# Changes of stage at 512 tokens: x and context accumulated in separate banks, x finished first, the next stage's first four tiles in two passes

## The reference

```python
for layer in range(2):
    x   = x   + 0.5 * mx[2] * swiglu(rms_norm(x)   * (1 + mx[1]) + mx[0], ffn1_gu, ffn1_down)
    ctx = ctx + 0.5 * mc[2] * swiglu(rms_norm(ctx) * (1 + mc[1]) + mc[0], ffn1_gu, ffn1_down)
    hx = rms_norm(x)   * (1 + mx[4]) + mx[3];   hc = rms_norm(ctx) * (1 + mc[4]) + mc[3]
    # hx @ w_in: q, k, v, pool, fft; hc the same (in the last layer only k, v)
    x   = x + mx[5] * (mixers(hx, hc) @ w_out)
    x   = x + 0.5 * mx[8] * swiglu(rms_norm(x) * (1 + mx[7]) + mx[6], ffn2_gu, ffn2_down)
    if layer == 0:
        ctx = ctx + mc[5] * (mixers(hc) @ w_out);   ctx = ctx + ... swiglu(...) as for x
# mx, mc = silu(c) @ ada_w + ada_b: the conditioning, nine groups a layer
```

## Time and profile before

| | us |
|---|---|
| median of 3 runs | 2786.44 |
| lowest, highest | 2783.71, 2787.35 |
| the profiled execution | 2785.05 |
| its span, first to last instruction | 2783.3 |

### The profile page before, as it was taken

One profiled execution on the slowest core, in us unless ns is written; L12 is line 12 of the kernel. 1 busy time (PEld: TensorE's weight loads), 2 busy tenths in 40 slices (PEclk: granted clock), 3 DMA queues, 4 the chain that ended last, 5 costly groups with the idle time before them and its releaser, 6 DMA issues. The chain is left out here.

```text
span 2783.3 us, 46152 instructions
## 1 busy us (share of the span) xinstructions
PE 2719.9 (98%) x17972; PEld 2430.3 (87%) x17972; DVE 1774.8 (64%) x2333; ACT 1202.5 (43%) x1757; POOL 202.1 (7%) x224
## 2 busy tenths in 40 slices
PE   7999999999999999999999999999999999999998
PEld 4888887788888878888879998999899999998998
DVE  4777535767772377742765568875476577668874
ACT  3233233642332232321555456554554445456553
POOL 1000012000000000000200014000200000004000
PEclk9999999999999999999999999999999999999999
DMA  6565532025663255543326643565456566653564
GB/s 255 189 189 189 166 108 76 16 94 190 190 187 104 83 161 190 187 143 98 123 103 196 197 155 110 177 202 176 146 178 204 177 202 216 202 175 109 183 200 136
DMA packets 153530, 444.07 MB, mean 160 GB/s; under 512 B 46528, under 2 KB 47936, under 8 KB 152768
## 3 DMA queue, kind: packets, MB, share of 16 engines
q1 hardware_dynamic: 119248, 431.38, 47.2%
q0 software_dynamic: 1008, 10.75, 1.0%
q10 hardware_dynamic: 33152, 0.26, 0.7%
HBM read 441.16 MB, written 1.18 MB: 159 GB/s over the span
## 5 line engine op out<-in xcount | busy, mean ns | idle before, releaser
L1726 DVE TENSOR_TENSOR wlo<-raw,whi 128x1024 fp32r<-128x1024 f32 x672 | 831.3, 1240 | 575.6 <-ACT whi L1220 572.8
L1220 ACT ACTIVATE whi<-raw 128x1024 fp32r<-128x1024 f32 x672 | 708.3, 1056 | 626.1 <-PE ps L573 575.4
L571 PE MATMUL ps<-nh,whi 128*128 128x512 f32 (+1 forms) x1280 | 498.4, 389 | 3.5 <-DVE nl L1791 1.7
L573 PE MATMUL ps<-nh,wlo 128*128 128x512 f32 (+1 forms) x1280 | 492.6, 385 | 0.0
L572 PE MATMUL ps<-nl,whi 128*128 128x512 f32 (+1 forms) x1280 | 492.6, 385 | 0.0
L571 PE MATMUL ps<-bh,whi 128*128 128x256 f32 x1456 | 405.9, 279 | 0.0
L572 PE MATMUL ps<-bl,whi 128*128 128x256 f32 x1456 | 404.6, 278 | 0.0
L573 PE MATMUL ps<-bh,wlo 128*128 128x256 f32 x1456 | 404.4, 278 | 0.0
L571 PEld LDWEIGHTS ps<-nh,whi 128*128 128x128 f32 x1280 | 241.2, 188 | 72.8 <-issue 12.6
L573 PEld LDWEIGHTS ps<-nh,wlo 128*128 128x128 f32 x1280 | 241.2, 188 | 48.1
L571 PE MATMUL ps<-mh,whi 128*128 (+1 forms) x1024 | 282.8, 276 | 0.0
(11 more groups left out here) (257 smaller groups left out, 4205.4 us busy)
## 6 DMA issues: line engine op xcount, KB each, us to landing
raw<-stream SPq DMA_DIRECT2D x800, 512.0 KB, 3.4
head<-stream SPq DMA_DIRECT2D x8, 1024.0 KB, 14.6
gates_w<-gate_in POOLq DMA_DIRECT2D x2, 3328.0 KB, 13.0
cst<-cst_in POOLq DMA_DIRECT2D x2, 1280.0 KB, 6.0
X<-x_in SPq DMA_DIRECT2D x1, 2048.0 KB, 7.8
out<-X SPq DMA_DIRECT2D x8, 128.0 KB, 2.0
fftw<-fftw_in POOLq DMA_DIRECT2D x2, 256.0 KB, 5.9
ws<-ws_in POOLq DMA_DIRECT2D x1, 512.0 KB, 3.9
```

The costliest lines, as they stand in the source:

```text
L571: pe.matmul(dst, w1, rhs_hi, start=start, stop=False)
L573: return pe.matmul(dst, w2, rhs_hi, start=False, stop=stop)
L1220: act.activation(whi[:, at % RING, :], raw[:, n % RING, :], ACT.Copy).then_inc(w_hi_ready, 1)
L1726: dve.tensor_tensor(wlo[:, r, :], raw[:, PLACE["main", at] % RING, :], whi[:, r, :].bitcast(F32), ALU.subtract).then_inc(w_ready, 1)
```

## The change

1. **Down and out projections at T** issue each 512-wide product as two 256-wide ones. `half_bank(m, half)` puts `x` of output tile m in banks 0 to 3, the context in banks 4 to 7, two tiles in one bank. A slot runs all eight tiles for one half, then for the other (`slot_halves`; the first slot of a stage takes the context half first).
2. **The last two slots** (`last_two_halves`) finish all `x` tiles first, then the context in the order `TURN[1]`. Between context tiles PE sums the squares of `x` and spreads its root.
3. **The norm** runs for `x`, then for the context (`norm_halves` on DVE and ACT, `norm_squares` on POOL), with the context's additions set between the scalings of `x`.
4. **The next stage's first four tiles** (`first_tiles`) run on `x` columns, with the context's sums and root between tiles, and then on context columns. In `in0` the conditioning's sums come between the passes, and ACT's store and load of it, with the wait between them, after the context's norm.
5. `keep_busy` is gone from these changes. `hh` and `hl` move from `WIDE_AT` to `NARROW_AT`; `nh` and `nl` stay.

```diff
-        hh = sb("hh", [P, NF * T], F32R, line=WIDE_AT)
-        hl = sb("hl", [P, NF * T], F32R, line=WIDE_AT)
+        hh = sb("hh", [P, NF * T], F32R, line=NARROW_AT)
+        hl = sb("hl", [P, NF * T], F32R, line=NARROW_AT)
...
+TURN = [list(range(KD)), [6, 7, 2, 3, 0, 1, 4, 5]]
+        ROW_BANK = [7, 5]
+        def half_bank(m, half):
+            return ps[:, 4 * half + m // 2, m % 2 * S:(m % 2 + 1) * S]
...
+            def first_tiles(at, widths, context_sums=True, between=None):
+                weights(at + 1)
+                for k in range(KD):
+                    pe.wait_ge(nl_ready, base + k + 1)
+                    for n in range(2):
+                        one(n, k, 0)
+                if context_sums:
+                    norm_sums(1, 6)
+                for n in (2, 3):
+                    weights(at + n)
+                    for k in range(KD):
+                        one(n, k, 0)
+                    if n == 2 and context_sums:
+                        norm_rows(1)
+                if between:
+                    between()
+                for k in range(KD):
+                    pe.wait_ge(nl_ready, base + KD + k + 1)
+                    for n in range(2):
+                        last = one(n, k, 1)
+                        if k == KD - 1:
+                            last.then_inc(slots_done, 1 if n == 0 or widths[2] == T else 3)
+                for n in (2, 3):
+                    if widths[n] == T:
+                        for k in range(KD):
+                            last = one(n, k, 1)
+                        last.then_inc(slots_done, 1)
...
+            def slot_halves(at, dyn, src_h, src_l, first, evac=None):
+                for half in ((1, 0) if first else (0, 1)):
+                    part = slice(half * S, (half + 1) * S)
+                    for m in range(KD):
...
+                        ins = mm3(half_bank(m, half), at, m, src_h[:, part], src_l[:, part],
+                                  first and m % 2 == 0, False)
+                ins.then_inc(slots_done, 1)
+            def last_two_halves(at, src):
+                for half in range(2):
+                    for i, m in enumerate(TURN[half]):
+                        for n, (src_h, src_l) in enumerate(src):
...
+                            if half and i == KD - 1:
+                                last.then_inc(slots_done, 1)
+                        if i % 2 and not (half and i == KD - 1):
+                            last.then_inc(acc_done, 1)
+                        if half and i == 3:
+                            norm_sums(0, 0)
+                        if half and i == 5:
+                            pe.wait_ge(x_new, done + KD + 2)
+                            norm_rows(0)
...
-                norm(T, busy=(9 if l else 6, 2, 11))
-                norm(w, busy=(13 if l else 9, 2, 6 if l else 11))
+                if w == S:
+                    norm((13, 2, 6))
...
+            def norm_halves(at, ord_shift, begun=False, ada=False):   # ACT
+                after = {0: [4], 1: [5], 3: [6], 4: [7]}
+                    for i in range(KD):
+                        square(i, T)
+                    for i in range(4):
+                        square(i, T, 1)
+                    root(0)
+                for m in range(KD):
+                        for i in after.get(m, []):
+                            square(i, T, 1)
+                    upper(m, ord_shift, nh)
+                    if m in (5, 6):
+                        split_to(at + m - 3)
+                    root(1)
+                for m in range(KD):
+                    upper(m, ord_shift, nh, 1)
+                if ada:
+                    ada_rows(c["ada"], 0, head_row)
+                    ada_columns(c["ada"], 0)
...
+            def norm_halves(at, ord_shift, scale_at, name=None, gate=None):   # DVE
+                if name:
+                    for i in range(KD):
+                        added(i, 0)
+                    add_last(0)
+                    for i in range(4):
+                        added(i, 1)
+                    inv_of_sums(0, 0)
+                    added(4, 1)
+                scaled(0, scale_at)
+                added(5, 1)
+                scaled(1, scale_at)
+                lower(0, ord_shift, nh, nl)
+                for m in range(2, KD):
+                    scaled(m, scale_at)
+                    lower(m - 1, ord_shift, nh, nl)
+                    if m in (2, 3):
+                        added(4 + m, 1)
+                    if m == 5 and name:
+                        add_last(1)
+                lower(KD - 1, ord_shift, nh, nl)
+                split_to(at + 2)
+                if name:
+                    inv_of_sums(1, 6)
+                split_to(at + 3)
+                for m in range(KD):
+                    scaled(m, scale_at, 1)
+                    if m:
+                        lower(m - 1, ord_shift, nh, nl, 1)
+                lower(KD - 1, ord_shift, nh, nl, 1)
```

More of the change, by code:

```diff
@@ L578, in keep_busy, with norm, norm_sums, norm_rows @@
                     pe.matmul(bank(b, P), ones[:], ident[:], start=True, stop=True)
[L580 to L587, removed]
+            def norm(busy, split=True):
+                pe.wait_ge(x_new, x_count(c["norm"]) + 2)
+                keep_busy(1, busy[0])
+                norm_sums(0, 0)
+                keep_busy(1, busy[1])
+                norm_rows(0)
+                keep_busy(1, busy[2])
+                c["norm"] += 1
+                c["nl"] += KD if split else 0
+            def norm_sums(half, b):
+                c["sums"] += 1
+                pe.wait_ge(all_added, c["sums"])
+                for n in range(2 * half, 2 * half + 2):
+                    last = pe.matmul(ps[:, b, n:n + 1], sqsum[:, n * P:(n + 1) * P], ones[:, 0:1],
+                                     start=True, stop=True)
+                last.then_inc(sq_summed, 1)
+            def norm_rows(half):
                 c["rms"] += 1
                 c["root"] += 1
-                keep_busy(1, busy[1])
                 pe.wait_ge(rstd_ready, c["root"])
[L592 to L607, removed]
+                spread(tok_rstd, 2 * half, ROW_BANK[half], half * S).then_inc(rows_ready, 1)
+            def spread(cols, first, b, at=0):
+                for n in range(2):
                     last = pe.transpose(ps[:, b, at + n * P:at + (n + 1) * P],
-                                        cols[:, n:n + 1].to_broadcast([P, P]), ident[:])
+                                        cols[:, first + n:first + n + 1].to_broadcast([P, P]), ident[:])
                 return last
@@ L703, in ffn_up, with group @@
                 if ada_groups:
-                    def group(at, unit, g, done, i, tiles=8):
-                        for n in range(tiles):
+                    def group(at, unit, g, done, i, tiles=8, first=False):
+                        if first:
+                            pe.wait_ge(up_evac, unit + 2)
+                            first_tiles(at, [T] * 4, context_sums=at > 0)
+                        for n in range(4 if first else 0, tiles):
                             q = n // 2
@@ L969, in channel_dft, with conditioning @@
                     last.then_inc(f1_done, 1)
-                joint_tiles(bank(0), in_slot(l, 0), bank(1), in_slot(l, 1), 0, T)
-                for i in range(1, 9):
-                    if i > 1:
+                def conditioning():
+                    ada_sums(c["ada"], ACC[KD * c["ada"]] + KD, 0)
+                    c["ada"] += 1
+                first_tiles(in_slot(l, 0), [T, T, w, w], between=conditioning if l == 0 else None)
+                for i in range(2, 9):
+                    if i > 3:
                         tile(i)
@@ L1515, in _ @@
             act.activation(csil[:, :, 0:2], cvec[:], ACT.Silu).then_inc(csil_ready, 1)
-            for m in range(KD):
-                square(m, T)
-            squared()
+            for half in range(2):
+                for i in range(KD):
+                    square(i, T, half)
             act.preload_act_table(ACT.Sqrt)
             ada_rows(0, 0, head_row)
-            root(T)
+            root(0)
+            root(1)
             split_to(1)
@@ new lines, in scaled @@
+            def scaled(m, scale_at, half=0):
+                part = slice(half * S, (half + 1) * S)
+                if m == 0:
+                    c["rows"] += 1
+                    dve.wait_ge(rows_ready, c["rows"])
+                elif m >= 2:
+                    dve.wait_ge(nl_ready, c["y"] + m - 1)
+                dve.scalar_tensor_tensor(
+                    out=tmpb[:, m % 2, part], in0=X[:, m, part], scalar=fix[:, scale_at, m, half:half + 1],
+                    in1=ps[:, ROW_BANK[half], part], op0=ALU.mult, op1=ALU.mult).then_inc(y_ready, 1)
```

314 lines of the change are left out of this document (187 added, 127 removed).

## The result

| | before | after |
|---|---|---|
| median, us (lowest to highest, 15 runs each) | 2786.44 (2782.39 to 2790.64) | 2789.92 (2788.42 to 2795.10) |
| ratio to before | 1 | 1.0019, 95% interval 1.0011 to 1.0027 |
| span of the profiled execution, us | 2783.3 | 2787.9 |
| mean granted clock in it | 0.992 | 0.998 |
| three matmuls on `hh` (before 512 wide, after 2 x 256) | 0.68 us | 2 x 0.353 us |

The account below looks back on a forecast made before the run. PE, busy 98% of the span, was taken as the bound. Savings of 2.1 + 0.1 + 1.0 + 0.4 - 1.0 = 2.6 us took the profiled 2785.05 to 2782.5, the median to 2784; range 2775 to 2792.

Parts of the forecast that it names:

- The halves of `down` at no cost: Three down projections: 3168 matmuls of 256 at 0.1133 us replace 1584 of 512, cost 0, at most +21 us.
- the halves of `down` aren't half: Rival, down projections: shared banks or register addresses slow the halves; at 0.120 a matmul 21 us lost, 2805; chance 0.05.
- the rule on the gap: Skill's gap of N/2.4 + 2.5 ns between matmuls: halving `down` would cost 4 us more; not used in the sum.
- One change of stage: `ffn1_up1`, from the start of the last two slots to tile three's end: 40.75 us instead of 42.87, 2.1 saved.
- DVE gets through sooner: Rival, changes of stage: the `x` pass takes 7.3 us, each of four changes saves 1.9 more, 2776; chance 0.18.
- `in0`: Stage change where the conditioning's sums, 1 us of PE, lay in the wait before and now between passes; 1.0 saved.
- Its queue of store and load on ACT: `in0`: store and 3.1 us load waited for in a row on ACT; delays PE by 0, at worst 2.5 us.
- `ffn2_up0`: Stage change after the out projection: 2.1 us saved, less 1.9 of `out0`, about 0.1 net.
- `out0`: Out projection: 384 matmuls of 256 on wide `nh` cost 2.56 us, 0.64 of it in a wait; 1.9 lost.
- `in1`: Stage change whose tiles 2 and 3 lack context columns: tile 6 ends at 47.0 instead of 47.4 us, 0.4 saved.
- The head: `ffn1_up0`, no down projection before it: joint tiles before taken to end at 51.72, tile three at 62.6, now 63.6; 1.0 us lost.
- The clock: Rival, four changes of stage: without `keep_busy` the clock dips at the wrong place, 1.4 us each, 5.6 lost, 2789.5; chance 0.12.

Follow-up runs that it names:

- e1: Kernel before, with the 512-token down slots issued as two 256-column passes, each tile in its own bank, `hh` and `hl` at the narrow place; 2796.27 us, ratio 1.0048.
- e2: Kernel after, with the tiles of a slot ordered so no two neighbours share a bank, except in a stage's last two slots; 2791.81 us, ratio 1.0030.
- e8: Kernel after, with six useless fp32 matmuls ahead of each of the three 512-token down projections; 2783.38 us, ratio 0.9995.
- e9: Kernel after, with one useless 512-column matmul on the narrow-placed `hh` ahead of each 512-token down projection; 2781.19 us, ratio 0.9985.
- e10: Kernel before, with one useless 512-wide matmul from a wide place ahead of each S-wide down projection; 2799.55 us, ratio 1.0059.
- e7: TensorE alone, computation left out: one thing put between 512-wide matmuls on wide-placed `nh` and narrow 256-wide ones; 0.1133 to 0.1178 us a matmul, by what lay between.
- e5: TensorE alone multiplying zeros, computation left out, only the moving rows' place varied; 256 columns take 0.1133 us at 64 bytes past a multiple of 256, 0.1200 at 128.

## Why the prediction was wrong, point by point

**The halves of `down` at no cost: the step that failed.** I took 0.1133 from `nh_s` and bounded it by 0.1200. The pace was 0.1178, between the two: 3168 x 0.0044 = 14 us, of which the table shows 12.8. My rival "the halves of `down` aren't half" named the right place, but gave `hh` 0.120, two mechanisms (a shared bank, which e1 and e2 exclude, and register addresses, which e8 excludes, since it keeps them and has 0.1133), and a chance of 0.05. What I did not see is that each row I priced from had its own predecessor: the narrow 256-wide stages of the kernel before follow 256-wide work, and the new ones follow the 512-wide tiles of an up projection without a gap. The row showed the cost of an operation in its sequence, and I moved it into another. That the predecessors do it is shown (e8, e9, e10); why they do stays open. That the time is inside the range all the same is luck: beside the 2.6 that was forecast, 1.7 more at the changes of stage and some 4 by the clock (both below) hid two thirds of the loss.

The prediction's remark that the rule on the gap speaks against the change was right in sign only. By it (the Trainium skill, TensorE: Matmul & The Clock Gate, section Back-to-back issue gap) the spacing of 256 columns is, as an estimate, 256/2.4 + 2.5 = 109.2 ns; the traces have 113.3, 117.8 and 120.0 for the same 256 columns, so the measurement decides. And in e8 two halves take exactly what one whole takes before (2 x 0.1133 against 0.2267), so the rule's 4 us are not what was lost.

**One change of stage.** Right, nearly term by term (forecast, measured): wait for the sums 1.15, 0.77; for the spread 0.4, none marked; for the first `nl` 0.7, 0.47; end of the `x` pass 22.6, 22.4; context pass without a wait, so; end of tile three 40.75, 40.45. The stretch with `ffn1_up1` won 2.4 where 2.1 was said. (My list of what remains of the 8.1 us is short by 0.2: two sums of 0.47 are 0.94, not 0.75. The 40.75 has them right.) DVE's chain does bind the `x` pass; "DVE gets through sooner" did not come, though its waits were a little shorter.

**`in0`** won 1.4 us where 1.0 was said: its tile five starts 49.38 us after the last two slots began before, 48.00 after. Its queue of store and load on ACT cost nothing. **`ffn2_up0`** won 2.4 and `out0` lost 1.9 (forecast 2.1 and 1.9). **`in1`** ends tile six 47.6 us after the start, where 47.0 was said and 47.4 is before: no gain. Tile four's weights are there at 38.7, where 38.3 was worked out, and PE idles 1.0 and 1.1 around the two matmuls on `kqs` (L1090, L979 in the kernel before; forecast 1.1 and 1.7):

```profile
1369.50 0.28 PE L589 MATMUL ps<-nh,wlo 128*128 128x256 f32 x1
1370.78 1.10 PE L1090 MATMUL ps<-kqs,cst 128*128 128x512 f32 x2 [1.00 <-ACT kqs L1624]
1372.98 0.36 PE L587 MATMUL ps<-nh,whi 128*128 128x256 f32 x1 [1.11 <-DVE wlo L1866]
```

**The head** lost nothing, where I had 1.0. The term was mis-sized on the side of before: I read 51.72 as the last feature's end, but it is the start of its six matmuls, so the joint tiles end at 53.08 and tile three at 63.96. After has it at 63.81, near my 63.6. The last rows of tile nine, before and then after:

```profile
96.37 0.39 PE L573 MATMUL ps<-nh,wlo 128*128 128x512 f32 x1
```

```profile
96.25 0.39 PE L589 MATMUL ps<-nh,wlo 128*128 128x512 f32 x1
```

**The clock** went the other way from my rival: the changes of stage of the kernel after show 1.00 where those of before show 0.81, as real work fills what `keep_busy` filled with gaps around it. The dips on useless matmuls cost before next to nothing; what counts is where useful ones ran at the lower clock. From 455 to 475 it was 0.83 before and 0.91 after (3.4 and 1.8 us lost), and with the 2.7 from 1578 on that makes some 4 us in this pair of executions. So 12.8 were lost, 4.3 won at the changes of stage and in the head (1.4 + 0.5 + 2.4 - 0.2 + 0.1, forecast 2.6), and some 4 by the clock, which leaves the 4.5 of the span. Part of the clock's 4 is this pair's own: the profiled execution of e9 had the lower clock back (0.94 from 1960 to 2020), and the means over all executions, above, differ by 0.0016 only.

**In sum** the plan of the change is worth what the prediction said once the pace is mended, as far as the noise lets one say so: e9 is 0.15% faster than before (interval 0.06 to 0.24%), 3.7 us on the medians, with 0.8 us paid for its three breaks; the forecast was 2.6.

## What to carry to other kernels

The price of a matmul is read from a row whose predecessors are those of the new place, not only its shape and address: the paces for the same 256 columns differ by 4% with what ran ahead (0.1133 and 0.1178), and by 6% with the place (0.1133 and 0.1200). Where halving or reordering puts narrow matmuls behind wider ones, look at the first hundred of them in the trace, and where they come slowly, try one useless matmul between, of the form that worked here (512 columns from a narrow place). Filling a wait with the real work of the other half did for the clock here what useless matmuls did before.

## What the runs showed of the hardware

- The pace of a stream of 256-wide fp32r matmuls has a memory: 0.1133 or 0.1178 us at the same addresses, held over 1032 matmuls in the stage and over 96 with nothing else running. A single 512-wide matmul on a wide place sets the slow one in the midst of narrow 256-wide ones (e7, e10), but not behind six fp32 ones or 96 wide ones of 256 (e7). One wide matmul of 384 columns, one narrow 512, 24 wide 256 or two fp32 ones lift it, one or three fp32 ones don't (e7), and on `mh` it went after five matmuls by itself (e10). Why is open.
- The first byte of the moving rows past a multiple of 256 sets the pace too: for 256 columns 64 is best (0.1133) and 128 worst (0.1200), for 512 columns 128 is best (0.2267 against 0.2333 at 64) (e5).
